# A hybrid attention, RWKV-7 and expert layer on one core: branch A's projection inside the scan steps, branch B by inner and outer chunks, triangles on four quarters

## The reference, cut to what matters

```python
h = rmsnorm(x, norm1_g) * (1 + sc1) + sh1
q, k, v, feat, gl = split(h @ w_in)
att = windowed_attention(q, k, v, sink) @ w_br_attn        # branch A
rw = rwkv7_bidir(feat, ...) @ w_br_rwkv                    # branch B
g_att, g_rw = split(sigmoid(gl))
x = x + gt1 * ((g_att * att + g_rw * rw) @ w_out)
h = rmsnorm(x, norm2_g) * (1 + sc2) + sh2
x = x + gt2 * expert_choice_moe(h, ...)                    # 16 experts
return rmsnorm(x, final_g)
```

## Time and profile before

| | |
|---|---|
| runs | 1598.31 us median of 3 (1594.44 to 1598.44) |
| the profiled execution | 1594.55 us, its span 1592.7 us |
| PE, DVE, ACT, POOL busy | 88%, 29%, 13%, 2% of the span |
| mean granted TensorE clock | 0.96 of full |
| chain that ended last | PE 57%, DMA 29%, DVE 8%, issue 3% |
| DMA | 485.5 MB, 305 GB/s over the span |
| scan, tail, output projection and routing | 411 to 504.5, 504.5 to 562.2, 562.2 to 649 us |

### The profile page before, as it was taken

The page is one execution under the profiler, slowest core; times in us unless marked ns, Lnnn a source line. Parts: engine busy times, 40 slices in busy tenths (PEclk is TensorE's granted clock), DMA queues, the critical chain, the costliest instruction groups (busy, mean ns, idle before and its releaser), DMA issues.

```text
span 1592.7 us, 21565 instructions
## 1 busy us (share of the span) xinstructions
PE 1402.1 (88%) x9239; PEld 663.4 (42%) x9239; DVE 467.1 (29%) x807; ACT 205.3 (13%) x401; POOL 39.1 (2%) x45
## 2 busy tenths in 40 slices
PE   5988999899778998799979889989889989889886
PEld 1433544445676444434334343344343343343332
DVE  3799643762237323310200200200200200201103
ACT  2024001122223002101001001001010010010002
POOL 2003030000000000000000000000000000000000
PEclk9998999999899999799999999999999999999998
DMA  9951242144402173799999999999999999999995
GB/s 346 374 174 58 80 106 63 56 135 118 174 5 112 76 279 127 279 428 429 427 428 429 428 428 429 428 428 428 428 430 428 429 429 428 428 429 428 428 428 209
DMA packets 91267, 485.52 MB, mean 305 GB/s; under 512 B 36075, under 2 KB 53565, under 8 KB 62405
## 3 DMA queue, kind: packets, MB, share of 16 engines
q1 hardware_dynamic: 91149, 484.59, 74.8%
q10 hardware_dynamic: 56, 0.01, 0.0%
HBM read 470.93 MB, written 10.50 MB: 302 GB/s over the span
## 4 chain that ended last, share of the span: by engine, by line
PE 57%; DMA 29%; DVE 8%; issue 3%; POOL 1%; ACT 1%; SPq 1%; DVEq 0%; PEldq 0%; POOLq 0%
PE psum L1111 16%; DMA arena<-in_exp_w_up_dram 14%; DMA arena<-in_exp_w_gate_dram 12%; PE psum L1126 8%; PE psum L694 6%; PE psum L581 5%; PE psum L1092 4%; DMA arena<-in_ada_w_dram 4%; PE psum L997 3%; PE psum L1027 3%; PE psum L1200 2%; DVE arena L1611 1%; PE psum L709 1%; DVE arena L1479 1%; DVE inv_tmp L1609 1%
## 5 line engine op out<-in xcount | busy, mean ns | idle before, releaser
L1111 PE MATMUL psum<-arena 128*64 128x512 f32 x2048 | 474.2, 620 | 81.2 <-DMA arena<-in_exp_w_up_dram 62.3
L1111 PEld LDWEIGHTS psum<-arena 128*64 128x64 f32 x2048 | 165.8, 142 | 382.7 <-issue 382.4
L1126 PE MATMUL psum<-arena 128*64 128x512 f32 x992 | 217.5, 596 | 11.2 <-issue 9.4
L581 PE MATMUL psum<-arena 128*128 128x512 f32 x336 | 149.1, 605 | 1.4 <-DVE arena L1505 1.4
L1126 PEld LDWEIGHTS psum<-arena 128*64 128x64 f32 x992 | 83.5, 138 | 139.5 <-issue 139.3
L694 PE MATMUL psum<-arena 128*128 128x512 f32 x256 | 124.5, 610 | 0.0
L581 PEld LDWEIGHTS psum<-arena 128*128 128x128 f32 x336 | 64.5, 194 | 84.2 <-issue 80.6
L1881 DVE TENSOR_TENSOR arena<-arena,psum 128x512 f32<-128x512 f32 x32 | 19.8, 681 | 268.5 <-PE psum L1111 268.5
L1896 DVE TENSOR_TENSOR arena<-psum,arena 128x1024 f32<-128x1024 f32 x7 | 8.6, 1225 | 251.3 <-PE psum L1126 251.3
L1873 DVE TENSOR_TENSOR arena<-arena,psum 128x512 f32<-128x512 f32 x32 | 19.8, 681 | 169.3 <-ACT arena L1422 169.3
L1413 ACT ACTIVATE arena<-psum,arena 128x128 f32<-128x128 f32 x64 | 24.3, 457 | 328.6 <-PE psum L1092 328.6
(11 more groups left out here) (269 smaller groups left out, 1067.7 us busy)
## 6 DMA issues: line engine op xcount, KB each, us to landing
arena<-in_exp_w_gate_dram SPq DMA_DIRECT2D x64, 2048.0 KB, 24.5
arena<-in_exp_w_up_dram SPq DMA_DIRECT2D x64, 2048.0 KB, 26.7
arena<-in_exp_w_down_dram SPq DMA_DIRECT2D x62, 2048.0 KB, 26.9
arena<-in_ada_w_dram SPq DMA_DIRECT2D x24, 1024.0 KB, 9.9
arena<-in_w_in_dram SPq DMA_DIRECT2D x16, 1024.0 KB, 5.8
arena<-in_x_dram SPq DMA_DIRECT2D x2, 2048.0 KB, 8.5
gate_pre<-arena SPq DMA_DIRECT2D x16, 256.0 KB, 6.1
arena<-in_w_out_dram SPq DMA_DIRECT2D x1, 4096.0 KB, 20.9
```

Source lines behind the costliest of these rows:

```text
L581: ins = mm(bank(b % 4), by(w_ring[g % 2], KC)[:, k, j * P:(j + 1) * P], by(hT, KC)[:, k, :], start=(k == 0), stop=(k == KC - 1))
L1111: ins = mm(bank(4 * kind + n)[e * 64:(e + 1) * 64, :], by(xeT, KC)[:, k, e * 64:(e + 1) * 64], by(ring[(j + e) % RING], 2)[:, r, n * 512:( ...
L1126: ins = mm(bank(4 + n)[e * 64:(e + 1) * 64, :], by(hidT, FBLK)[:, 4 * kk + b, e * 64:(e + 1) * 64], by(ring[(j + e) % RING], 4)[:, b, n * ...
```

## The change

It does five things:
1. projection block 9 is put ahead of `kk_sum`;
2. the triangle products alternate between the directions, so that four consecutive ones use four quarters of the array, each bank holding one direction of two chunks in the order 4, 5, 6, 7, 4, ...; two gate products follow every pair of banks, eight in all;
3. attention takes 24 gate products a block instead of 26, the head transpose of a block comes inside the next one, and the inversion is dealt out anew (`inverse`), a part of it behind the logits;
4. branch A's products 0 to 27 are put into scan steps 1 to 7, four a step, with bank 7, DVE's gating in the next step and two sigmoids on ACT in steps 1 and 2; the transposed keys of both directions share bank 6;
5. branch B is split: inner chunks 2 to 5 for groups 0 to 4 while the outer ones are still scaled, then the outer chunks, then groups 5 to 7 whole. Two mix operations a group. wbr is loaded once the scan's last C product is done, to another place.

The diff, cut to its core:

```diff
 SP
-                sp.wait_ge(sem("A_made"), 4 * d + 4)
+                sp.wait_ge(sem("A_made"), 7 + d)
...
             load(by(gate_half[0], KC), gate_rows[:, 0:KC, :], "gates_in")
+            load(GG, g_spill, "g_moved")
+            sp.wait_ge(sem("C_mm"), 2 * STEPS)
+            sp.wait_ge(sem("N_mm"), 2 * STEPS - 2)
+            load(by(wbr, 4), w_br_rwkv[0].rearrange("(k p) n -> p k n", p=P), "wbr_in")
             load(by(gate_half[1], KC)[:, 0:4, :], gate_rows[:, KC:KC + 4, :], "gates_in")
-            load(GG, g_spill, "g_moved")
             sp.wait_ge(sem("Y_mm"), STEPS)
             load(by(gate_half[1], KC)[:, 4:KC, :], gate_rows[:, KC + 4:GATEB, :], "gates_in")
-            load(by(wbr, 4), w_br_rwkv[0].rearrange("(k p) n -> p k n", p=P), "wbr_in")
 PE
-            for b in range(7, 9):
+            for b in range(7, 10):
                 project(b)
...
+            def a_product(d, n, c, m, h):
...
+                return mm(bank(4 + (2 * n + d) % 4)[head(p), o:o + CHUNK], left[head(h), d, m, token(c)],
...
+            for n in range(4):
+                if n >= 2:
+                    pe.wait_ge(sem("A_made"), 2 * n - 2)
...
+                            a0 = a_product(0, n, c, m, h)
+                            a1 = a_product(1, n, c, m, h)
...
+                gate_products(2 * n, 2 * n + 2)
...
-                g0 = 26 * q
+                g0 = 8 + 24 * q
+                ahead, doubled = ((6, 2), (6, 2), (6, 2), (4, 0))[q]
...
+                    if q and j == 1:
+                        heads_turned(q - 1)
...
-                gate_products(g0 + 22, g0 + 26)
...
-                return mm(cell(6 + d, slot(h, d), m, 256 * n), (be_, ka_)[n][head(h), d, m, token(chunk(i, d))],
+                return mm(cell(6, slot(h, d), m, 256 * n), (be_, ka_)[n][head(h), d, m, token(chunk(i, d))],
...
+            def att_branch(b, m, k):
+                if k == 0 and b == 7 and m:
+                    pe.wait_ge(sem("mixT_ready"), m)
+                ins = mm(bank(b), by(wba, 4)[:, k, m * P:(m + 1) * P], by(attT, 4)[:, k, :], start=(k == 0), stop=(k == 3))
+                if k == 3:
+                    ins.then_inc(sem("mix_mm"), 1)
...
                 if not last:
                     Bq(i + 1)
+                if i == 1:
+                    pe.wait_ge(sem("wba_in"), 16)
+                if i:
+                    att_branch(7, i - 1, 0)
                 U(i, 1)
                 U(i, 0)
                 if not last:
                     C_with_turns(i + 1)
                 if i > 5:
                     gn_transposed(i - 2)
+                if i:
+                    att_branch(7, i - 1, 1)
                 if not last:
                     SU(i)
+                if i:
+                    att_branch(7, i - 1, 2)
                 Y(i)
                 if i < STEPS - 2:
                     transposed(i + 1, 1)
+                if i:
+                    att_branch(7, i - 1, 3)
...
+            for k in range(4):
+                att_branch(5, 7, k)
             gn_transposed(6)
+            pe.wait_ge(sem("Y_out"), STEPS)
+            pe.wait_ge(sem("wbr_in"), 16)
+            pe.wait_ge(sem("gn_out"), 2)
+            for m in range(3):
+                rw_branch(m, "inner")
             gn_transposed(7)
+            rw_branch(3, "inner")
+            pe.wait_ge(sem("gn_out"), 3)
+            rw_branch(4, "inner")
             pe.wait_ge(sem("gn_out"), 4)
             for m in range(KC):
+                if m > 5:
+                    pe.wait_ge(sem("mixT_ready"), m + 1)
+                rw_branch(m, "outer" if m < 5 else "all").then_inc(sem("mix_mm"), 1)
 ACT
+                if i in (1, 2):
+                    act.wait_ge(sem("gates_in"), 16)
+                    gate_sigmoid(0, i - 1)
...
+            act.wait_ge(sem("gates_in"), 48)
+            for n in range(2):
+                gate_sigmoid(1, n)
 DVE
+            def inverse(k):
...
+                lo = 2 * k + 1 if k < 4 else k + 4 if k < 21 else 2 * k - 17
+                for i in range(lo, lo + (2 if k < 3 or k > 20 else 1)):
+                    invert(i)
...
+                    if q in (1, 2) and n % 2:
+                        inverse(12 * (q - 1) + n // 2)
...
                     if q in (1, 2):
-                        if (q, h) == (1, 0):
-                            dve.wait_ge(sem("tri_in"), 16)
-                        for i in range(16 * q + 2 * h - 15, 16 * q + 2 * h - 13):
-                            if i < HALF - 1:
-                                invert(i)
+                        inverse(12 * (q - 1) + 4 + h)
...
+            def att_gated(m, b):
+                dve.wait_ge(sem("gate_ready"), 1 + m // 4)
+                dve.wait_ge(sem("mix_mm"), m + 1)
+                v.tensor_tensor(ga[:, m, :], ga[:, m, :], bank(b), ALU.mult).then_inc(sem("mixT_ready"), 1)
+
             for i in range(STEPS):
                 last = i == STEPS - 1
+                if i > 1:
+                    att_gated(i - 2, 7)
...
+            att_gated(6, 7)
+            att_gated(7, 5)
             for m in range(KC):
...
-                s(v.tensor_tensor(mix_tmp[0], ga[:, m, :], bank(m if m < 6 else m - 4), ALU.mult))
-                s(v.tensor_tensor(mix_tmp[1], gr[:, m, :], bank(6 + m % 2), ALU.mult))
-                v.tensor_tensor(by(mixT, KC)[:, m, :], mix_tmp[0], mix_tmp[1], ALU.add).then_inc(sem("mixT_ready"), 1)
+                s(v.tensor_tensor(mix_tmp, gr[:, m, :], bank((0, 1, 2, 3, 6, 4, 7, 5)[m]), ALU.mult))
+                v.tensor_tensor(by(mixT, KC)[:, m, :], mix_tmp, ga[:, m, :], ALU.add).then_inc(sem("mixT_ready"), 1)
```

More of the change, by code:

```diff
@@ L621, in _ @@
             ins.then_inc(sem("kk_sum"), 1)
-            for b in range(9, 12):
+            for b in range(10, 12):
                 project(b)
@@ L658, in _ @@
             pe.wait_ge(sem("beta_ready"), 1)
[L659 to L681, removed]
             def gate_products(lo, hi):
@@ L728, in _ @@
                         transpose_probs(h + 1)
-                    gate_products(g0 + 14 + h, g0 + 15 + h)
+                    more = 2 if h < doubled else 1
+                    gate_products(g0, g0 + more)
+                    g0 += more
                     if h == 0 and q:
@@ L737, in _ @@
                     ins.then_inc(sem("pv_mm"), 1)
-                gate_products(g0 + 22, g0 + 26)
[L739 to L744, removed]
+            gate_products(100, 104)
+            heads_turned(TT - 1)
             Tv = Tt.rearrange("p (d x t) -> p d x t", d=DIRS, x=32)
@@ L991, in _ @@
                     transposed(i + 1, 1)
-            def branch(w, src, b, m):
-                for k in range(4):
-                    right = rw_cols[:, k] if src is None else by(src, 4)[:, k, :]
-                    ins = mm(bank(b), by(w, 4)[:, k, m * P:(m + 1) * P], right, start=(k == 0), stop=(k == 3))
-                return ins
-            rw_cols = y_rw.rearrange("p (c m t) -> p m c t", c=STEPS, m=PAIRS)
-            pe.wait_ge(sem("wba_in"), 16)
-            branch(wba, attT, 0, 0)
+                if i:
+                    att_branch(7, i - 1, 3)
@@ new lines, in _, with rw_branch @@
+            rw_in = y_rw.rearrange("p (c m t) -> p m c t", c=STEPS, m=PAIRS)
+            RWB = (0, 1, 2, 3, 6, 4, 7, 5)
+            def rw_branch(m, cols):
+                for k in range(4):
+                    b, left = bank(RWB[m]), by(wbr, 4)[:, k, m * P:(m + 1) * P]
+                    if cols == "inner":
+                        ins = mm(b[:, 2 * CHUNK:6 * CHUNK], left, rw_in[:, k, 2:6], start=(k == 0), stop=(k == 3))
+                    elif cols == "all":
+                        ins = mm(b, left, rw_in[:, k], start=(k == 0), stop=(k == 3))
+                    else:
+                        for e in range(2):
+                            o = 6 * e
+                            ins = mm(b[:, o * CHUNK:(o + 2) * CHUNK], left, rw_in[:, k, o:o + 2],
+                                     start=(k == 0 and e == 0), stop=(k == 3 and e == 1))
+                return ins
@@ L1297, in _ @@
                        accum_out=ast[:, 4, h:h + 1]).then_inc(sem("probs_ready"), 1)
-                    if h == 2:
-                        gate_out((0, 4, 7, 10)[q])
-                for idx in ((1, 2), (5,), (8,), (11, 12))[q]:
+                    if h == 2 and q < 3:
+                        gate_out(3 * q + 2)
+                for idx in ((3,), (6,), (9,), (11, 12))[q]:
                     gate_out(idx)
@@ L1329, in T_out @@
                 act.wait_ge(sem("N_mm"), after(i, d))
-                fn(by(BK[i % 2], 2)[:, d], bank(6 + d), ACT.Copy).then_inc(sem("N_out"), 1)
+                fn(by(BK[i % 2], 2)[:, d], bank(6), ACT.Copy).then_inc(sem("N_out"), 1)
             def gn_square(j):
@@ L1339, in gn_root, with gate_sigmoid @@
                 fn(gn_stat[:, 16:24], gn_stat[:, 8:16], ACT.Sqrt).then_inc(sem("gn_std"), 1)
+            def gate_sigmoid(half, part):
```

(2 more changed lines are left out.)

93 lines of the change are left out of this document (51 added, 42 removed).

## The result

The changed kernel takes **1579.29 us** (median of 5 runs, 1578.48 to 1585.02) against 1598.31 for the kernel before (median of 5, 1594.44 to 1599.21). The ratio is 0.9894, with a 95% interval of 0.9872 to 0.9916: faster by 1.1%, between 0.8 and 1.3%. The forecast was 1583.5, with a range from 1573 to 1592.5.

The account below looks back on a forecast made before the run. PE bounds the part ahead of the DMA-full expert loop, so savings there come off the end. Front -11.4 and scan with tail -3.3 make -14.7 from the profiled 1594.55; 3.8 carried over gives 1583.5 us, range 1573 to 1592.5.

Parts of the forecast that it names:

- Part 1, +2.5: Projection 9 ahead of the kk sums: no time won, the hole moves and projections behind start at half clock, +2.5 us.
- Parts 2 and 3, -13.9: Triangles and attention: eight gate products earlier -6.9, half clock at 238 gone -1.7, copy waits -6.7, uncovered transposing copy +1.4.
- L1658's exposure: Attention: without four gate products behind block 2 the transposing copy is uncovered, and PE waits for block 3's logits, +1.4 us.
- Rival (a): Scan: only the semaphore waits absorb products, not the mid-batch holes; 10.7 us more, 1594 us, chance 0.09.
- The products cost 0.862: Branch A in the scan steps: each product taken at 0.862 us, so 24 in steps 1 to 6 add 20.7 us before absorption.
- The sigmoids +4.9: Scan steps 1 and 2: ACT's two sigmoids stand between the keys' copy and Y's copy, on the chain, +4.9 us.
- The loads of step 6, +3: SP's loads of wbr and gates (3 MB) while PE streams instructions may cause holes and half clock, +3 us (0 to 7).
- Step 7, wait 2.5: Scan step 7: first product waits 2.5 us for DVE's gating of group 5; with four products' 3.4, +5.9 us.
- +5.7: Scan steps 1 to 6: what remains of 24 branch A products after holes and waits absorb them, +5.7 us (0 to 16.4).
- (c): The front gives nothing: DVE stays late in attention and early gate products only lengthen the waits; 1597 us, chance 0.06.
- (b): Scan: sigmoids stretch the waits in steps 1 and 2, and two steps run at half clock; 1607 us, chance 0.04.
- (d): Everything is absorbed in the scan, and projection 9's move and step 6's loads are free; 1572 us, chance 0.1.

Follow-up runs that it names:

- sig_mid: Changed kernel with ACT's two gate sigmoids of scan steps 1 and 2 moved between the two copies of transposed keys: 1573.93 us, ratio 0.9869 to the kernel before.
- gated_early: Changed kernel with DVE's gating of group 5 put ahead of the scaling of the first outer chunk pair: 1576.22 us, ratio 0.9870 to the kernel before.
- front_only: Kernel before with only the projection, triangle and attention changes, scan and tail as before: 1580.79 us against 1597.45, ratio 0.9889.
- rephase_64: Kernel before with 64 more PE instructions (one batch of key transposes repeated) ahead of scan step 0: 1596.34 us, one run.
- two_products: Changed kernel with only the first and last of branch A's four products in each scan step: 1570.09 us, one run.
- p1_back: Changed kernel with projection 9 put back behind the kk sums: 1578.68 us, ratio 0.9901 to the kernel before.

## Why the prediction was right

The forecast was 14.7 us, and the spans differ by 15.1. It isn't as close as that in its parts: the front gave 2.1 us more than forecast and the scan with the tail 1.4 less, and the rest is the first and last stretch. By its steps:

**Part 1, +2.5.** Measured +2.45 (1.5 in the projections, 0.95 in kk_spread), and -2.4 with the move undone. That no time is won where DVE's reciprocal ends last, and that the hole takes the clock with it, was right.

**Parts 2 and 3, -13.9.** From the first triangle to the scan it took 193.15 us (217.95 to 411.10) and takes 177.21 (218.48 to 395.69): -15.9. The eight early products, the half clock of 238, and L1658's exposure (+1.4 forecast, 1.6 measured) came as worked out, the first with a shortfall. PE reached the first scores at 233.94 and not at 232.4. Half a microsecond of that is the later start of the triangles. The quarters go at 1.10/64 = 0.017 us an instruction, not 0.015, which is 0.6 us for all of them, and the eight gate products in pairs take 7.6 us, not 6.9. PE has no wait left there, so both count. More than that came back in blocks 1 and 2. With two gate products fewer each they take 33.4 and 33.5 us (from the first scores of one to those of the next) instead of 40.0 each, 13.1 less together. The four gate products are 3.4 of it, the waits for DVE all of their 7.8, of which I had left 1.1. The other 1.9 us no row here explains.

**Part 4.** The mechanism holds: the mid-batch holes are the instruction stream's, and products fill them. These runs disagree with the rule of the Trainium skill's "Runtime: NRT & Kernel Launch", section "Instruction fetch mechanics", that fetching is hidden behind the issue floor: here it costs 9 us of the scan before, L808's 13.3 without step 0's 4.3. Rival (a) is out. Four terms were sized wrongly, in both directions. *The products cost 0.862*: they cost 1.05 among 64x64 products, 0.19 more, 4.6 us over 24 of them, and the batch behind pays too. *The sigmoids +4.9*: their holes are 5.0, and the clock behind them 1.5 more; sig_mid measured 6.6 in all. *The loads of step 6, +3*: close to nothing, near the bound that I had named. The hole at that place is 0.36 us and stands in front of the wait for DVE; without two of the products it is 2.6. *Step 7, wait 2.5*: 1.8, but half clock behind it, 3.2 together by gated_early. From the scan's start to the end of Y_out(6) it came to +14.2 (87.25 to 101.43), where the terms +5.7, +4.9 and +3 make 13.6. That their sum was closer than its parts is luck. Without the sigmoids' 6.5 us it is 7.7 for the 24 products, 0.3 each of the 1.05 that one takes. They take 25.3 us, so 17.6 of it went into waits, where I had 15.0; that and the loads, which cost next to nothing, made up for the dearer products and the clock. From there to Y's end it came to +6.7 (6.17 to 12.85), where +5.9 was forecast for step 7.

**Part 5, the tail.** 35 us were forecast from Y's end, 34.9 measured. The outer columns cost 0.112 us an instruction rather than 0.124, so +0.3 instead of +1.3; gn_out 4 held nothing up, as forecast.

**Carrying over the 3.8 us** between the median and the profiled execution of before was a choice without a mechanism. The changed kernel's profiled execution is itself the median of its runs (1579.29), and 1579.8 without the carry would have been nearer.

**Rivals.** (c) is refuted by front_only, (a) by rephase_64 and two_products. (b) occurs in part: 3.45 us halved the clock, as it feared, 2.03 did not in the changed kernel's trace but did in gated_early's, and the price was an eighth of what I gave a step. (d) half: the loads were close to free, the rest not.

What stays open: the 1.9 us of blocks 1 and 2 beyond the waits; why a hole of one length halves the clock in one execution and not in another, which makes 1.3 of the 1.9 us between the changed kernel's scan stretch and that of p1_back; and how much of the front's gain is the triangles' and how much attention's, since no run has one without the other.

## What to carry to other kernels

Look for holes in the middle of a batch of small matmuls: if they move when instructions are added ahead of them, PE waits for its own instructions, and long products put there cost about a third of their own time (0.3 to 0.4 us of 1.05 here). They have to be spread over the step: four in one place brought the holes back, and pairs were hardly faster than single ones once the other waits were gone (1566.82 and 1566.87 us). Before a hidden operation is moved to another engine's loop, find the copy in that loop that the next step waits for, and put the operation ahead of an idle stretch, not ahead of that copy. And split a change into its halves early: here one half gave nearly all of it, and the other hid 6.6 us of gain behind two misplaced sigmoids.

## What was not expected of the hardware

- A 128x128 by 128x512 product takes 0.862 us in a row of its kind, 1.05 alone between 64x64 products, and the 64 instructions of 64x64 behind it 1.09 instead of 0.93. Two in a row take 1.91.
- Holes of the same length, 2.03 us in step 2, cost the clock in one execution (0.50 at 448 to 450 in gated_early) and not in another (1.00 in the changed kernel's). So did one of 1.85 us in p1_back, and one of 2.9 in front_only (0.50 at 478 to 480), where the same hole of the kernel before left the clock full.
- PE stalls at borders of 127 matmuls with their weight loads when the matmuls are small, 0.4 to 1.9 us each in quiet stretches and 3.2 to 4.3 under full DMA load in step 0, and each stall ends 1.2 to 1.6 us behind the landing of a 16 KB instruction packet.
- DMA at full load did not slow PE's instructions where long products stood among them: 492 to 496 us of the changed kernel at 369 GB/s, with PE busy 4.00 of 4 us at the full clock.
